# First RMSNorm statistics placed between the adaLN blocks, and GLA gate weights loaded in the prologue, in a two-layer hybrid decoder trunk

## The reference, cut to what matters

```
c_act = silu(c)
mod = c_act @ ada_w[i] + ada_b[i]                 # 1024 x 6144
shift_t, scale_t, gate_t, shift_c, scale_c, gate_c = split(mod, 6)
h = x * rsqrt(mean(x*x, -1) + 1e-6) * norm_g[i,0] * (1 + scale_t) + shift_t
y = gla_mixer(h, ...)    # layer 0; layer 1: differential attention
x = x + gate_t * y
h = rmsnorm(x, norm_g[i,1]) * (1 + scale_c) + shift_c
x = x + gate_c * (square(relu(h @ mlp_w1[i])) @ mlp_w2[i])
```

## Time and profile before

| quantity | value |
|---|---|
| time, median of 2 runs | 2842.41 us (2841.07 to 2843.76) |
| time of the profiled execution | 2838.74 us |
| its span, slowest core (core 5) | 2837.5 us |
| spans of the 8 cores | 2825.5 to 2837.5 us |
| mean granted TensorE clock, by core | 0.846 to 0.851 |
| TensorE busy | 2160.9 us (76%) |
| VectorE busy | 1178.8 us (42%) |
| ScalarE busy | 976.4 us (34%) |
| GpSimd busy | 181.3 us (6%) |

### The profile page before, as it was taken

One profiled execution on the slowest core, in us unless ns is written; L12 is line 12 of the kernel. 1 busy time (PEld: TensorE's weight loads), 2 busy tenths in 40 slices (PEclk: granted clock), 3 DMA queues, 4 the chain that ended last, 5 costly groups with the idle time before them and its releaser, 6 DMA issues.

```text
span 2837.5 us, 31281 instructions; the slowest of 8 cores (2825.5 to 2837.5 us)
## 1 busy us (share of the span) xinstructions
PE 2160.9 (76%) x9898; PEld 956.0 (34%) x9898; DVE 1178.8 (42%) x1560; ACT 976.4 (34%) x1756; POOL 181.3 (6%) x168
## 2 busy tenths in 40 slices
PE   3347767774999999945686878677787749999994
PEld 1113323331344444412332423243243304444441
DVE  0033444334433343436553554465365434443444
ACT  0164343435402021162363246145435553112113
POOL 0000000000000000002200400400140000000000
PEclk8668888885999899966887989888798859999996
DMA  9900011003044423130000100100100011112003
GB/s 187 199 8 1 1 30 30 1 4 56 4 66 76 67 57 60 30 60 0 1 1 0 31 1 1 30 1 1 30 1 1 1 30 30 30 30 41 19 1 119
DMA packets 8146, 94.93 MB, mean 33 GB/s; under 512 B 898, under 2 KB 1155, under 8 KB 1331
## 3 DMA queue, kind: packets, MB, share of 16 engines
q0 software_dynamic: 5184, 75.50, 15.4%
q1 hardware_dynamic: 2804, 17.43, 1.8%
HBM read 160.03 MB, written 8.39 MB: 59 GB/s over the span
## 4 chain that ended last, share of the span: by engine, by line
PE 65%; DVE 12%; ACT 9%; issue 6%; DMA 4%; POOL 2%; another core or an unknown queue 1%; DVEq 0%; ACTq 0%; POOLq 0%; SPq 0%
PE ps L397 16%; PE ps L379 16%; PE ps L810 4%; PE ps L852 4%; DMA wsl<-wblk 4%; PE ps L813 4%; PE ps L787 4%; DVE xTs L856 3%; PE ps L721 3%; PE ps L611 2%; PE ps L482 2%; PE ps L763 2%; ACT hTs L364 2%; PE ps L345 2%; ACT U L343 2%
## 5 line engine op out<-in xcount | busy, mean ns | idle before, releaser
L379 PE MATMUL ps<-hTs,wsl 128*128 128x512 bf16 x2048 | 457.4, 387 | 8.6 <-DVE U L387 5.0
L397 PE MATMUL ps<-U,wsl 128*128 128x512 bf16 x2048 | 443.3, 379 | 0.0
L797 ACT ACTIVATE U<-ps 128x512 bf16<-128x512 f32 (+3 forms) x640 | 324.6, 532 | 321.7 <-PE ps L792 155.2
L385 ACT ACTIVATE U<-ps 128x512 f32<-128x512 f32 x256 | 152.6, 597 | 470.6 <-PE ps L379 466.4
L401 DVE SCALAR_TENSOR_TENSOR xTs<-ps,modv,xTs 128x512 f32<-128x512 f32 x256 | 192.1, 751 | 244.6 <-PE ps L397 244.6
L387 DVE SCALAR_TENSOR_TENSOR U<-ps,U 128x512 bf16<-128x512 f32 x256 | 176.6, 691 | 281.1 <-ACT U L385 281.1
L379 PEld LDWEIGHTS ps<-hTs,wsl 128*128 128x128 bf16 x2048 | 203.3, 99 | 260.5 <-issue 38.9
L397 PEld LDWEIGHTS ps<-U,wsl 128*128 128x128 bf16 x2048 | 200.4, 98 | 241.6
L810 PE MATMUL ps<-U 128*128 128x512 bf16 (+3 forms) x640 | 232.7, 364 | 44.2 <-ACT U L797 23.0
L813 PE MATMUL ps<-U,onesb 128*128 128x512 bf16 (+3 forms) x640 | 231.7, 362 | 0.0
L787 PE MATMUL ps<-U 128*128 128x512 bf16 (+3 forms) x640 | 231.1, 365 | 0.0
(11 more groups left out here) (127 smaller groups left out, 2138.2 us busy)
## 6 DMA issues: line engine op xcount, KB each, us to landing
wsl<-wblk POOLq DMA_DIRECT2D x36, 2048.0 KB, 16.4
xTs<-xT SPq DMA_DIRECT2D x8, 1024.0 KB, 74.7
outT<-xTs SPq DMA_DIRECT2D x8, 1024.0 KB, 11.6
cstf<-cst SPq DMA_DIRECT2D x1, 256.0 KB
U<-wa SPq DMA_DIRECT2D x1, 192.0 KB, 2.4
U<-wa SPq DMA_DIRECT2D x1, 96.0 KB, 2.1
sms<-sm SPq DMA_DIRECT2D x1, 80.0 KB
lrow<-rw SPq DMA_DIRECT2D x1, 1.0 KB
```

The lines of the kernel that those rows point to most:

```text
L379: P.add("pe", lambda e, ps=ps, w1=w1, k=k, j=j, ts=ts: e.matmul(ps[:], w1[:, k * 1024 + j * 128:k * 1024 + (j + 1) * 128], hT[:, k, ts], s ...
L385: P.add("act", lambda e, ps=ps, sq=sq: e.activation(sq, ps[:], AF.Square), reads=[psr], writes=[sqr])
L397: P.add("pe", lambda e, ps=ps, w2=w2, j=j, dch=dch, ts=ts: e.matmul(ps[:], w2[:, j * 1024 + dch * 128:j * 1024 + (dch + 1) * 128], hid[:, ...
L797: P.add("act", lambda e, ps=ps, pT=pT, n0=n0: e.activation(pT[:, n0:512], ps[:, n0:512], AF.Exp, scale=0.125), reads=[psr], writes=[pTr])
```

## The change

1. The loads and casts of `wa` and `wa2` leave `gla` and stand in the prologue, after the constants and before silu(c). They write the same columns of `U` as before. The two loads come behind the eight pieces of x on SP's queue, the two casts behind the constants on VectorE, and all of them ahead of the fence that precedes the adaLN blocks.
2. The norm's statistics become a function `norm_stats`. For the first norm all four calls stand between adaLN blocks 2 and 3, and write into one area `rstd_all` at column 12288 of `U`.
3. The first `norm` is then called with `pre=True` and without its fence: only L361's and L364's work is left in it.
4. In the other norms `n_rstd` becomes one resource per token block, with an alias barrier between them, because they share one buffer.

```diff
--- before.py
+++ after.py
@@ -292,6 +292,14 @@
               reads=[R("cstf"), R("cstb")], writes=[R("cstb")])
         P.add("dve", lambda e: e.memset(onesb[:], 1.0), writes=[R("onesb")])
         P.add("dve", lambda e: e.memset(onesf[:], 1.0), writes=[R("onesf")])
+        g_wab = Ub(2048, 384)
+        g_wa2b = U[0:48, 2432:2944]
+        g_waf = Uf(2944, 384)
+        g_wa2f = U[0:48, 3712:4736].bitcast(F32)
+        P.add("sp", lambda e: e.dma_start(out=g_waf, in_=wa_d), writes=[R("waf")], dma=True)
+        P.add("sp", lambda e: e.dma_start(out=g_wa2f, in_=wa2_d), writes=[R("wa2f")], dma=True)
+        P.add("dve", lambda e: e.tensor_copy(g_wab, g_waf), reads=[R("waf")], writes=[R("wab")])
+        P.add("dve", lambda e: e.tensor_copy(g_wa2b, g_wa2f), reads=[R("wa2f")], writes=[R("wa2b")])
         P.add("act", lambda e: e.activation(cact[:], sm[:, SM_C:SM_C + 8], AF.Silu),
               reads=[R("sm")], writes=[R("cact")])
 
@@ -331,36 +339,46 @@
         NO = 29400 - 5120
         UEND = 29400
 
-        def norm(gs_ap, sh_ap, final=False, fence=True):
+        rstd_all = Uf(12288, 2048)
+
+        def norm_stats(tb, out_rstd):
+            ts = slice(tb * 512, (tb + 1) * 512)
+            pss, pssr = ps_next([0, 1])
+            for k in range(8):
+                sq = Ub(NO + (k % 2) * 512, 512)
+                sqr = R("n_sq", k % 2)
+                P.add("act", lambda e, sq=sq, k=k, ts=ts: e.activation(sq, xT[:, k, ts], AF.Square),
+                      reads=[R("x", k, tb)], writes=[sqr])
+                P.add("pe", lambda e, pss=pss, sq=sq, k=k: e.matmul(pss[:], onesb[:], sq, start=(k == 0), stop=(k == 7)),
+                      reads=[sqr, R("onesb")], writes=[pssr])
+            lnt = Uf(NO + 1024, 512)
+            P.add("act", lambda e, pss=pss, lnt=lnt: e.activation(lnt, pss[:], AF.Ln, bias=EPS, scale=1.0 / D),
+                  reads=[pssr], writes=[R("n_ln")])
+            P.add("act", lambda e, lnt=lnt, out_rstd=out_rstd: e.activation(out_rstd, lnt, AF.Exp, scale=-0.5),
+                  reads=[R("n_ln")], writes=[R("n_rstd", tb)])
+
+        def norm(gs_ap, sh_ap, final=False, fence=True, pre=False):
             if fence:
                 P.fence()
             for tb in range(4):
                 ts = slice(tb * 512, (tb + 1) * 512)
-                pss, pssr = ps_next([0, 1])
-                for k in range(8):
-                    sq = Ub(NO + (k % 2) * 512, 512)
-                    sqr = R("n_sq", k % 2)
-                    P.add("act", lambda e, sq=sq, k=k, ts=ts: e.activation(sq, xT[:, k, ts], AF.Square),
-                          reads=[R("x", k, tb)], writes=[sqr])
-                    P.add("pe", lambda e, pss=pss, sq=sq, k=k: e.matmul(pss[:], onesb[:], sq, start=(k == 0), stop=(k == 7)),
-                          reads=[sqr, R("onesb")], writes=[pssr])
-                lnt = Uf(NO + 1024, 512)
-                rstd = Uf(NO + 2048, 512)
-                P.add("act", lambda e, pss=pss, lnt=lnt: e.activation(lnt, pss[:], AF.Ln, bias=EPS, scale=1.0 / D),
-                      reads=[pssr], writes=[R("n_ln")])
-                P.add("act", lambda e, lnt=lnt, rstd=rstd: e.activation(rstd, lnt, AF.Exp, scale=-0.5),
-                      reads=[R("n_ln")], writes=[R("n_rstd")])
+                if pre:
+                    rstd = rstd_all[:, ts]
+                else:
+                    rstd = Uf(NO + 2048, 512)
+                    P.alias_barrier([R("n_rstd", t_) for t_ in range(4) if t_ != tb], [R("n_rstd", tb)])
+                    norm_stats(tb, rstd)
                 for k in range(8):
                     if final:
                         P.add("dve", lambda e, k=k, ts=ts, rstd=rstd: e.scalar_tensor_tensor(
                             xT[:, k, ts], xT[:, k, ts], gs_ap[:, k:k + 1], rstd, ALU.mult, ALU.mult),
-                            reads=[R("n_rstd"), R("sm")], writes=[R("x", k, tb)])
+                            reads=[R("n_rstd", tb), R("sm")], writes=[R("x", k, tb)])
                     else:
                         tmp = Uf(NO + 3072 + (k % 2) * 1024, 512)
                         tr = R("n_tmp", k % 2)
                         P.add("dve", lambda e, k=k, ts=ts, rstd=rstd, tmp=tmp: e.scalar_tensor_tensor(
                             tmp, xT[:, k, ts], gs_ap[:, k:k + 1], rstd, ALU.mult, ALU.mult),
-                            reads=[R("n_rstd"), R("x", k, tb), R("dv")], writes=[tr])
+                            reads=[R("n_rstd", tb), R("x", k, tb), R("dv")], writes=[tr])
                         P.add("act", lambda e, k=k, ts=ts, tmp=tmp: e.activation(
                             hT[:, k, ts], tmp, AF.Identity, bias=sh_ap[:, k:k + 1]),
                             reads=[tr, R("modv")], writes=[R("h", k, tb)])
@@ -437,10 +455,6 @@
             sqb = [Ub(o + i * 512, 512) for i in range(2)]; o += 1024
             assert o <= UEND, o
 
-            P.add("sp", lambda e: e.dma_start(out=waf, in_=wa_d), writes=[R("waf"), R("modrow")], dma=True)
-            P.add("sp", lambda e: e.dma_start(out=wa2f, in_=wa2_d), writes=[R("wa2f"), R("modrow")], dma=True)
-            P.add("dve", lambda e: e.tensor_copy(wab, waf), reads=[R("waf")], writes=[R("wab")])
-            P.add("dve", lambda e: e.tensor_copy(wa2b, wa2f), reads=[R("wa2f")], writes=[R("wa2b")])
             for tb in range(4):
                 ts = slice(tb * 512, (tb + 1) * 512)
                 ps, psr = ps_next([0, 1])
@@ -883,10 +897,14 @@
                 w_issue()
 
         P.fence()
-        for nb_ in range(6):
+        for nb_ in range(3):
+            adaln_block(0, nb_)
+        for tb in range(4):
+            norm_stats(tb, rstd_all[:, tb * 512:(tb + 1) * 512])
+        for nb_ in range(3, 6):
             adaln_block(0, nb_)
         adaln_finish(0)
-        norm(dv[:, 0:8], modv[:, 0:8])
+        norm(dv[:, 0:8], modv[:, 0:8], fence=False, pre=True)
         gla()
         if stage >= 2:
             norm(dv[:, 8:16], modv[:, 24:32])
```

## The result

The changed kernel takes 2826.46 us (median of 26 runs) beside 2841.24 for the kernel before (25 runs). The medians count every execution, while the ratios compare only undisturbed ones: the ratio is 0.9933, 95% interval 0.9915 to 0.995. On another chip it is 0.9938 (0.9923 to 0.9953). A ratio of 0.9933 is 19 us less: within 2%, and clear of no change. 10.6 us had been forecast. The profiled execution took 2820.51 us.

A forecast was written before the change was run, and what follows sets the result against it. Loads, then the norm's chain on ScalarE and VectorE, were taken to bound the head. The terms put GLA's start at 182.7 instead of 193.3, 10.6 us off the runs' median 2842.41: 2831.8 us, range 2823 to 2843.

The forecast's parts named there:

- steps 3 and 5: In the head, adaLN blocks 0 to 2 and 3 to 5 take 8.3 us each, 24.9 us per three.
- step 1: In the head, x's five remaining pieces load alone at 3.6 us each, complete at 72.6 us (bounds 69.1 to 73.6).
- Steps 1 and 2: In the head, x then `wa` and `wa2` (1.5 us) land, the second cast takes 0.42 us, TensorE starts at about 74.7.
- Step 4: In the first norm, four token blocks of statistics sum to 31.1 us, to 130.7; TensorE is free at 129.4.
- step 6: First norm's application: sixteen pairs take 26.7 us plus 0.6 for the tail, to 182.5; GLA's first matmul at 182.7.
- Rival (a): At the first fence: gate weights land before x and do not hold it; gain 4.6, time 2837.8 us; chance 0.07.
- Rival (b): In the head: x alone keeps its 15.9 us spacing, complete at about 134, time 2893 us; chance 0.04.
- Rival (c): Whole kernel: the head gets shorter but the end does not, the slowest core giving it back; 2842 us; chance 0.11.

The follow-up runs named there:

- the kernel held by x: Changed kernel with gate weights loaded and cast in GLA, first fence held by a one-column VectorE copy of x's last piece: ratio 0.9965, again 0.9971.
- the spread one: Changed kernel with layer 1's six adaLN blocks one by one behind w1 and w2 of the first three MLP groups: ratio 0.9893.

## Why the prediction was right or wrong

The mechanism was right in each step; the size was not. On core 7 GLA started at 174.78, where 182.7 was forecast. The terms, in their order:

| step | forecast us | measured us |
|---|---|---|
| 1 and 2, TensorE's start | 74.7 | 71.32 |
| 3, adaLN blocks 0 to 2 | 24.9 | 23.1 (94.41 - 71.32) |
| 4, statistics until TensorE is free | 29.8 | 29.0 (123.42 - 94.41) |
| 5, adaLN blocks 3 to 5 | 24.9 | 22.7 (144.22 + 1.91 - 123.42) |
| 5, bias add and finish | 0.9 | 0.9 |
| 6, application and fence | 27.5 | 27.7 |

The step that failed is the price of an adaLN block, in steps 3 and 5, together with step 1's price of a piece of x; no wait, overlap or path was wrong.

Steps 3 and 5 took 8.3 us a block, from L305's mean of 5.55 and the words "a run without DMA waits does not shorten it". It does. On core 7 the six are 6.21, 5.14, 3.62, 4.08, 5.30 and 5.22, mean 4.93, and with the rest of a block 7.6 us. Over all cores the mean is 4.88 where it was 5.65 before. The two errors come to 1.8 + 2.2 = 4.0 us. The length follows TensorE's granted clock, as two windows of these blocks show:

```profile
80.31:85.40 5.09, 5.09 (x17) 1.55 (x16) 0.17 (x1) 0.59 (x1) 0.00 (x0) 0.69 1.08 180
...
88.12:91.70 3.58, 3.58 (x17) 1.26 (x16) 0.17 (x1) 0.59 (x1) 0.00 (x0) 1.00 0.90 146
```

At 0.88 it took 4.08 us, and at 0.67 and 0.68 it took 5.30 and 5.22. The first block does not fit: 6.21 us, though its window shows 1.00. I had left the clock out of this term. The two rows that I had for a second block, 5.30 and 6.52, were from the slow side; in the same trace the first block of each of these two pairs took 3.61.

Steps 1 and 2 were 3.4 us too long. On core 7 five pieces of x alone took 15.5 us, 3.1 each, where I took 3.6: 2.5 us less. The third piece was in at 53.5 instead of 54.6, 1.1 us less, and the gate weights took 2.3 us for 2.1. The write-out row had said 2.9 and the hardware queue's share 3.5; the measured price lies between them, and I had leaned on the higher one. That share was poor evidence, probably because most of x's packets were timed while they shared the engines with weight blocks. The kernel with x first comes out close, at 3.2 to 3.3 us a piece.

The Trainium skill (DMA: Bandwidth & Descriptors, Specifications) puts the limit at about 358 GB/s, 2.9 us a piece. The 338 GB/s measured here are 6% below it.

The sum of the three errors is 3.4 + 1.8 + 2.2 = 7.4 of the 7.9 us; all went one way. The forecast bounds reached them only at their very edge (a gain of 1 to 18 us, 18.2 measured as a mean), and the chosen point lay in the middle of ranges whose ends were tied to single rows. The prediction also took 57 us as about what a measurement of this kernel can tell from no change; the interval of the ratio is 5 us to either side.

Step 4 and step 6 held within a microsecond. Blocks 3 to 5 hid under the statistics, with 4 us to spare and not 12: by its packets block 3 was in 16.7 us after it was sent, where 12.1 had been taken. The norms' alias barriers cost nothing that shows: GLA to the end is no longer than before.

That the fence would be held by the cast of `wa2` was the decisive reading, and the experiments bear it out: without it the head gains 9.9 us instead of 18.2, and holding without the statistics gains 1.7. It is the pair that works. Rival (a) was the kernel with the casts in GLA, priced at 188.7 and measured at 183.2 (183.7 on its slowest core). There too the adaLN term is the larger error: blocks 3 to 5 took 20.5 us for 24.9, and x was complete at 107.9 for 109.7. Rival (b) fell at the first DMA window: x alone ran faster. Rival (c), that the end does not follow the head, did not happen to this change, but did in part to its neighbour: the kernel held by x kept 8 to 10 of 16.5 us. The difference is slower matmuls behind the first MLP; what makes them slower stays open.

## What to carry to other kernels

Before you price a moved load, ask what its first consumer stands in front of: a cast that nobody needs yet, placed ahead of a fence, holds every engine, and here decided about half of the result. Held alone, without work that could use the time, it gave next to nothing. Where a stage is bound by loads, sort them by what can start when they land; x ahead of the weights, and the use of h as soon as its two vectors are there, made four times the original change's gain, with that change in it. Where small blocks follow one another in a ring of slots, spread them: here two in a row cost the next large block its time to load. And measure the end as well as the head: from the GLA start the same work took 2635 to 2641 us, as a mean over the cores, in kernels that differ in nothing but the head.

## What was not expected of the hardware

The same 256 matmuls of a w1 phase took from 55.43 to 59.23 us in the changed kernel and always 55.43 in the spread one. On core 7 two of the long ones begin with TensorE's granted clock at 0.50, one behind a load wait of 4.51 us and one behind none. Taking away 5.3 to 5.9 us of waits (means over cores) with the pairs of adaLN blocks shortened the stretch from GLA to the end by 9 to 11 us, to 2626.4, and brought that stretch within 3.3 us on the eight cores, where it had been 16 to 18 apart. Waits and clock together are what the order of the blocks was worth; which part of the clock's loss belongs to the waits is not shown.
